# Seven block products in a second tile of a hybrid attention and recurrence kernel, with the weight sums made by accumulating DMAs

## The chip, the cores and the metric

The kernel runs on one core of a Trainium2 chip, in one launch. The metric is the device time in microseconds of that core, the median of three runs; one more execution was profiled. The engines are TensorE (PE), VectorE (DVE), ScalarE (ACT), GpSimd (POOL) and SyncE (SP), which only issues DMAs here.

## The reference

One block of a streaming encoder over `x` (1, 2048, 1024), all in float32. Eight attention heads with 2 key heads, over a window of two chunks of 64 positions, with sinks; four heads of a gated linear recurrence (HGRN2) with a 128 x 128 state; each branch gated by SiLU:

```python
h = rmsnorm(x, w_norm_pre[l])
proj = h @ w_in[l]                                   # 1024 -> 3328 = 26 * 128
q_a, k_a, v_a, z_a, q_r, f_r, i_r, z_r = jnp.split(proj, SPLIT_POINTS, axis=-1)
...
o_a = sliding_window_sink_attention(q_a, k_a, v_a, attn_sinks[l]) * jax.nn.silu(z_a)
...
o_r = hgrn2_chunkwise(q_r, f_r, i_r, lb)
o_r = rmsnorm(o_r, hgrn_norm[l]).reshape(B, S, HGRN_WIDTH) * jax.nn.silu(z_r)
y = jnp.concatenate([o_a, o_r], axis=-1) @ w_out[l]  # 1024 -> 1024
x = x + rmsnorm(y, w_norm_post[l])
```

## The kernel before

**Tiles and steps.** The sequence is cut into four tiles of 512 positions (`TILES`, `N`), numbered 0 to 3, worked one after the other. A tile has 26 weight tiles of 128 output columns for the input projection (key, value, 4 query, 4 gate, and forget, query, value, gate of each of four heads) and then the output projection, whose weight is 8 more weight tiles (`OUT0` to `WT` = 34). Each engine runs through the same numbered steps `s`, one per weight tile, and does the part of attention or recurrence that is due; `between` (L729) places TensorE's small matmuls among the products.

**Split weights and operands.** A float32 product is made of three matmuls of float32r operands: high by high, low by high, high by low (`products`, L591). So each weight tile (512 KB) has a high and a low half. ScalarE makes the high half (`split_hi`, L919), VectorE the low half (`split_lo`, L1257) from the raw tile that SyncE loaded (`load_raw`, one of 4 slots of `w_raw`). A weight tile of the input projection is 24 matmuls.

**Keeping the halves.** `SPLIT_SLOT` says in which of 4 slots of `w_hi`, `w_lo` a weight tile lies; the last six of tile 0 use slots 0, 1, 2 alone. With `LATE` = 6, the first six weight tiles are split in tile 0 without being saved; those from 6 on are saved to DRAM (`save_split`, `kept_hi` and `kept_lo`); the first six of tile 1 are loaded raw and split again, and saved then. From `FRESH` = 40 on, `load_split` (L461) loads both halves back. It waits that TensorE has finished with the slot (`wait_slot`) and that the slot's saves have landed (`wait_saved`, L379). SyncE's program is in order, so whatever follows a wait in it waits too; at each weight tile it comes to: raw load, save of the tile four back, load of kept halves, then x, tables, sums, residual, stores.

**Two forms of the output projection.** Tiles 0 and 1 (`t < FAST`, FAST = 2) multiply plainly: 8 weight tiles x 24 = 192 matmuls of 512 columns (`out_plain`). Tiles 2 and 3 use a 2 x 2 block form with seven products rather than eight: 56 units x 3 = 168 matmuls (`out_fast`, `UNITS`). It needs sums of activation blocks (`sum_head`, `a_sum`; VectorE), their high and low parts, and eight further weight tiles T1 to T4, which are sums of blocks of the output weight. These are made once: SyncE loads four raw tiles, VectorE subtracts them four times (`sum_weights`, L1453), ScalarE rounds them to high halves that lie in `mix_hi`, `mix_lo` (`sums_high`), VectorE makes the low halves, SyncE saves both. The first four are made at the end of tile 1, the other four in steps 5 to 8 of tile 2.

**Attention.** In step 8, 10, 12, 14 TensorE computes the scores of a pair of chunks (`scores`), VectorE takes the maximum and writes `probs` (`softmax_first`, L1426), ScalarE the exponent, VectorE sums and scales it one step later (`softmax_sums`, L1434), and TensorE transposes it two steps after the scores (`turn`, L643).

**End of a tile.** After a plain tile ScalarE squares the output, VectorE and GpSimd scale it and add the residual, and ScalarE issues five DMAs that store it (`PLAIN_STORES`, L1232). GpSimd issues no DMA.

Of the kernel before, what the change touches and what calls it, by code (L numbers as in the profile page):

```python
# [49 lines left out]
OUT0 = H0 + 4 * HEADS  # L50
WT = OUT0 + KT
# [10 lines left out]
FAST = 2  # L62
# [6 lines left out]
SPLIT_SLOT += [w % 4 for w in range(WT)] + [(WT + w) % 4 for w in range(FAST_WT)] * (TILES - FAST)  # L69
assert WT == 34 and OUT0 == 26 and FAST_WT % 4 == 0 and FAST == 2  # L70
# [40 lines left out]
SUMS_IN = (FAST - 1, H0 + 8), (FAST, 5)  # L111
SUMS_OUT = ((FAST, 0, 0), (FAST, 1, 2)), ((FAST, H0, 0), (FAST, H0 + 2, 2))
SUMS_AT = 5
# [39 lines left out]
LATE = 6  # L153
# [36 lines left out]
def hybrid_block(nc, x, x_rows, weights, cos, sin, vectors, w_post, squares, out, kept):  # L190
# [3 lines left out]
    with ctx:  # L194
# [3 lines left out]
        def sem(name):  # L198
# [32 lines left out]
        t_probs = nc.alloc_sbuf_tensor_at("t_probs", [P, 2, 2, N], FP32R, offset=probs_at)  # L231
        t_more = nc.alloc_sbuf_tensor_at("t_more", [P, 2, 2, N], FP32R, offset=raw_at + 4 * RAW_SLOTS * KT * P)
# [38 lines left out]
        t_hi = [t_more[:, 0, :, :], t_probs[:, 1, :, :], t_more[:, 1, :, :], t_probs[:, 0, :, :]], \  # L271
               [mix[:, 2 * i:2 * i + 2, :] for mix in (mix_hi, mix_lo) for i in range(2)]
# [32 lines left out]
        stored = [sem(f"stored{i}") for i in range(2)]  # L305
# [38 lines left out]
        t_raw, t_sum, t_high, t_low, t_saved = (sem(n) for n in ("t_raw", "t_sum", "t_high", "t_low", "t_saved"))  # L344
# [27 lines left out]
        def wait_raw(engine, i):  # L372
            engine.wait_ge(w_loaded[i % RAW_SLOTS], 16 * (i // RAW_SLOTS + 1))

# [58 lines left out]
        def _(sp):  # L433
            def load_x(tile, k):


                if k == 0:
                    sp.wait_ge(h_lo_done.sem, h_lo_done.after(tile - 1, -1))
                    sp.wait_ge(x_squared.sem, x_squared.after(tile - 1, -1))
                    sp.wait_ge(finished.sem, finished.after(tile - 2, -1))  # L440
                    sp.wait_ge(finished_pool.sem, finished_pool.after(tile - 2, -1))
                sp.dma_start(x_in[:, k:k + 2, :],
                             x[bass.ts(tile, P), k * N:(k + 2) * N].rearrange("p (k n) -> p k n", n=N)).then_inc(x_quarter[k // 2], 16)
# [17 lines left out]
            def load_split(tile, w):  # L461
# [4 lines left out]
                if w == P7A and tile == FAST:  # L466
                    sp.wait_ge(t_saved, 16 * 2 * T_TILES)
# [4 lines left out]
            def load_sums(j):  # L472

                if j == 0:
                    sp.wait_ge(lo_split.sem, lo_split.after(0, 0) + FRESH - 1)
                else:
                    sp.wait_ge(t_saved, 16 * T_TILES)
                for r, w in enumerate((B11, B21, B12, B22)):
                    sp.dma_start(w_raw[:, r, :, :], weights[(w + j) * P:(w + j + 1) * P, :].rearrange("p (k m) -> p k m", k=KT)).then_inc(t_raw, 16)

            def save_sums(j, first):

                sp.wait_ge(t_high, 4 * j + first + 2)
                sp.wait_ge(t_low, 4 * j + first + 2)
                for r, w in ((0, T1), (2, T3)) if first == 0 else ((3, T2), (1, T4)):
                    rows = slice((w + j) * P, (w + j + 1) * P)
                    sp.dma_start(kept[0][rows, :].rearrange("p (k m) -> p k m", k=2), t_hi[j][r].bitcast(FP32)).then_inc(t_saved, 16)
                    sp.dma_start(kept[1][rows, :].rearrange("p (k m) -> p k m", k=KT), w_raw[:, r, :, :]).then_inc(t_saved, 16)
# [44 lines left out]
            for t in range(TILES):  # L533
                for w in range(tiles_of(t)):
# [12 lines left out]
                    if w - H0 in range(0, KT, 2) and t + 1 < TILES:  # L547
                        load_x(t + 1, w - H0)
                    if w == OUT0 and t + 1 < TILES:
                        load_tables(t + 1)  # L550
                    if (t, w) in SUMS_IN:
                        load_sums(SUMS_IN.index((t, w)))
                    for j in range(2):
                        for first in (0, 2):
                            if (t, w, first) in SUMS_OUT[j]:
                                save_sums(j, first)
# [10 lines left out]
            sp.wait_ge(stored[0], 32 * TILES + 48)  # L567
            sp.wait_ge(stored[1], 48 * TILES + 32)
# [336 lines left out]
        def _(act):  # L905
# [98 lines left out]
            def sums_high(k):  # L1004

                act.wait_ge(t_sum, k + 1)
                if k == 4:
                    act.wait_ge(t_saved, 16 * T_TILES)
                r = (0, 2, 3, 1)[k % 4]
                act.activation(t_hi[k // 4][r], w_raw[:, r, :, :].rearrange("p k m -> p (k m)").rearrange("p (k n) -> p k n", k=2), ACT.Copy).then_inc(t_high, 1)  # L1010
# [30 lines left out]
            for t in range(TILES):  # L1041
                links[0] = 0
                for s in range(WT):
# [63 lines left out]
                    for head in range(HEADS):  # L1107
                        if s == out_step(head) + 2:
                            act.wait_ge(head_mixed.sem, head_mixed.after(t, head))
                            act.activation(mix_hi[:, QT + head, :], h_mix[:, :], ACT.Copy).then_inc(mixh_hi.sem, 1)  # L1110
                        if t >= FAST and s == out_step(head) + (3 if head < HEADS - 1 else 2):
                            act.wait_ge(s_made.sem, s_made.after(t, head))
                            if t == FAST and head == 0:
                                act.wait_ge(t_saved, 16 * 2 * T_TILES)
                            act.activation(s_hi[:, :, head, :], s_tmp, ACT.Copy).then_inc(s_high.sem, 1)
                    if t == FAST and s in (SUMS_AT + 1, SUMS_AT + 2):
                        for k in range(2):
                            sums_high(4 + 2 * (s - SUMS_AT - 1) + k)
# [15 lines left out]
                    for head in range(HEADS):  # L1134
                        if s == out_step(head):
# [4 lines left out]
                            act.wait_ge(o_done.sem, o_done.after(t, head))  # L1140
                            act.activation(o_sq_hi, out_b, ACT.Square)
# [27 lines left out]
                    if t >= FAST and s in MIXA:  # L1169
                        first = MIXA[s][0] == 0  # L1170
                        act.wait_ge(gated.sem, gated.after(t, PAIRS - 1)) if first else act.wait_ge(a_sum.sem, a_sum.after(t, 0))
                        if t == FAST and first:
                            act.wait_ge(t_saved, 16 * 2 * T_TILES)
# [9 lines left out]
                    if s == OUT0 + 4 and t < FAST:  # L1183
                        for b in range(4):
                            square_y(t, 0, b)
                        for k in range(4) if t == FAST - 1 else ():
                            sums_high(k)
# [34 lines left out]
                if t + 1 < TILES:  # L1222
# [4 lines left out]
                    for b, cols, pieces, pool_pieces in PLAIN_STORES if t < FAST else ():  # L1227

                        act.wait_ge(finished.sem, finished.after(t, pieces - 1))
                        if pool_pieces:  # L1230
                            act.wait_ge(finished_pool.sem, finished_pool.after(t, pool_pieces - 1))
                        act.dma_start(out[bass.ds(t * N + b * P, P), cols[0] * N:(cols[-1] + 1) * N].rearrange("p (h n) -> p h n", n=N),  # L1232
                                      q_gate[:, 2 * b + cols[0]:2 * b + cols[-1] + 1, :]).then_inc(stored[b // 2], 16)
# [4 lines left out]
        def _(dve):  # L1238
# [77 lines left out]
            def rope_turn(t, r):  # L1316
# [14 lines left out]
                else:  # L1331
                    dve.wait_ge(stored[0], t * 32 + 32)
# [71 lines left out]
            def softmax_first(t, q):  # L1404
# [15 lines left out]
                dve.wait_ge(turned.sem, turned.after(t, q - 1))  # L1420
                if t == 0 and q == 0:
# [22 lines left out]
            def sum_head(t, h):  # L1444
# [3 lines left out]
                dve.tensor_tensor(s_tmp[:, S2, :], h_mix[:, 2 * P:], s3[:, h, :], ALU.subtract).then_inc(s_step, 1)  # L1448
# [361 lines left out]
```

## Time and profile before

| | |
|---|---|
| runs | 864.86 us median of 3 (864.5 to 866.69) |
| the profiled execution's own time | 864.57 us |
| its span, first to last instruction | 862.7 us |
| granted TensorE clock | 0.999 of full |
| TensorE busy | 851.9 us (99%) |
| VectorE busy | 631.9 us (73%) |
| ScalarE busy | 519.0 us (60%) |
| GpSimd busy | 114.6 us (13%) |
| DMA | 211.20 MB, mean 245 GB/s |

Busy is the time in which an engine works on an instruction; matmuls overlap one another in it (one of 512 columns is shown with 0.39 us, and the next begins 0.23 us after it). All times below are counted from the first instruction of the span. A tile has 816 such matmuls, or 792 with seven products, and runs for some 210 us.

### The profile page before, as it was taken

Reading aid. Unit: us, or ns where it says so; the run is one execution under the profiler, and the core shown is the slowest. Engines: PE = TensorE matmul, PEld = TensorE weight load, DVE = VectorE, ACT = ScalarE, POOL = GpSimd, SP = SyncE. Lnnn points to the kernel's source line nnn. Section 1 sums busy time; section 2 is a strip of 40 time slices with the busy share of each in tenths; the row PEclk is TensorE's granted clock in tenths of the full one; section 3 lists DMA queues with packets and bytes.
Section 4 is the critical chain, followed back from the end, with each engine's and each line's share of the span. In section 5 each row is a group of like instructions: output and inputs, shape, how many; then the busy total and the mean of one; then the engine's idle time right before and its main releaser. Section 6 shows DMA issues by size and latency. Waiting matters only on the chain.

```text
span 862.7 us, 12445 instructions
## 1 busy us (share of the span) xinstructions
PE 851.9 (99%) x4428; PEld 700.6 (81%) x4428; DVE 631.9 (73%) x1125; ACT 519.0 (60%) x1033; POOL 114.6 (13%) x84
## 2 busy tenths in 40 slices
PE   8999999999999999999999999999999999999997
PEld 6787788888888778888888878888888887888885
DVE  6878878674656799767747789887775368888846
ACT  7766445763466458567446655865853755576544
POOL 0000013430200000332020000144300000004220
PEclk9999999999999999999999999999999999999999
DMA  8686755748986647464898785445699674444586
GB/s 322 212 325 221 244 205 170 285 147 314 418 342 248 213 145 265 152 210 133 321 382 348 276 330 172 146 151 216 241 374 396 228 273 147 147 147 158 189 326 254
DMA packets 59981, 211.20 MB, mean 245 GB/s; under 512 B 6672, under 2 KB 6928, under 8 KB 59920
## 3 DMA queue, kind: packets, MB, share of 16 engines
q1 hardware_dynamic: 57904, 205.56, 65.3%
q10 hardware_dynamic: 2016, 4.85, 1.4%
q8 instruction: 35, 0.57, 0.3%
q14 instruction: 26, 0.21, 0.1%
HBM read 157.95 MB, written 52.43 MB: 244 GB/s over the span
## 4 chain that ended last, share of the span: by engine, by line
PE 84%; DVE 9%; ACT 4%; issue 3%; DVEq 0%
PE bank L596 55%; PE bank L605 5%; PE turn_b L852 3%; PE score_b L852 3%; PE bank L852 3%; PE score_b L605 3%; PE turn_b L605 3%; PE turn_b L653 2%; DVE kv_tok L1386 2%; PE score_b L629 2%; PE turn_b L706 2%; PE bank L697 1%; PE bank L687 1%; PE turn_b L709 1%; ACT probs_t L951 1%
## 5 line engine op out<-in xcount | busy, mean ns | idle before, releaser
L596 PE MATMUL bank<-h_hi,w_lo 128*128 128x512 f32 x832 | 326.9, 393 | 0.0
L596 PE MATMUL bank<-h_lo,w_hi 128*128 128x512 f32 x832 | 326.3, 392 | 0.0
L596 PE MATMUL bank<-h_hi,w_hi 128*128 128x512 f32 x832 | 324.4, 391 | 0.5 <-issue 0.5
L596 PEld LDWEIGHTS bank<-h_lo,w_hi 128*128 128x128 f32 x832 | 156.4, 188 | 34.7 <-issue 3.3
L596 PEld LDWEIGHTS bank<-h_hi,w_hi 128*128 128x128 f32 x832 | 156.4, 188 | 33.1 <-issue 1.0
L596 PEld LDWEIGHTS bank<-h_hi,w_lo 128*128 128x128 f32 x832 | 156.3, 188 | 32.8
L1716 POOL TENSOR_TENSOR mix_lo<-v_r,mix_hi 128x512 fp32r<-128x512 f32 x16 | 21.2, 1322 | 539.0 <-ACT v_r L1142 539.0
L1263 DVE TENSOR_TENSOR w_lo<-w_raw,w_hi 128x1024 fp32r<-128x1024 f32 x36 | 44.8, 1248 | 34.6 <-ACT w_hi L924 34.1
L1386 DVE STREAM_TRANSPOSE kv_tok<-k_mid 32x128 f32<-32x128 f32 x192 | 58.1, 303 | 2.8
L924 ACT ACTIVATE w_hi<-w_raw 128x1024 fp32r<-128x1024 f32 x38 | 39.8, 1051 | 24.9 <-issue 10.2
L1700 POOL TENSOR_TENSOR x_acc<-x_acc,x_sq 128x512 f32<-128x512 f32 x21 | 32.7, 1557 | 70.0 <-ACT x_sq L974 70.0
L928 ACT ACTIVATE g_a<-g_b 128x512 f32<-128x512 f32 x30 | 18.9, 630 | 38.2 <-DVE g_b L1340 38.2
L939 ACT ACTIVATE g_a<-g_a 128x512 f32<-128x512 f32 x32 | 20.2, 632 | 34.6 <-DVE g_a L1344 34.6
L1068 ACT ACTIVATE f_b<-bank 32x512 f32<-32x512 f32 x48 | 28.3, 589 | 15.6 <-PE bank L596 9.7
L960 ACT ACTIVATE kv_tok<-f_d 32x128 f32<-32x128 f32 x96 | 29.5, 307 | 10.0 <-DVE f_d L1580 8.9
L1344 DVE SCALAR_TENSOR_TENSOR g_a<-g_b,g_a 128x512 f32<-128x512 f32 x30 | 21.7, 723 | 18.3 <-ACT g_a L930 18.3
L960 ACT ACTIVATE probs<-f_d 32x128 f32<-32x128 f32 x96 | 29.5, 307 | 1.2
L1637 DVE TENSOR_TENSOR_SCAN f_c<-reset,f_b 128x512 f32<-128x512 f32 x16 | 19.6, 1225 | 11.3 <-ACT f_b L1125 11.3
L1479 DVE SCALAR_TENSOR_TENSOR q_gate<-q_gate,y_stats,x_in 128x512 f32<-128x512 f32 x28 | 23.1, 873 | 4.4 <-DMA x_in<-in_x_rows 3.5
L605 PE MATMUL bank<-w_hi,mix_lo 128*128 128x512 f32 x64 | 25.3, 395 | 0.0
L605 PE MATMUL bank<-w_hi,mix_hi 128*128 128x512 f32 x64 | 24.9, 390 | 0.0
L605 PE MATMUL bank<-w_lo,mix_hi 128*128 128x512 f32 x64 | 24.9, 389 | 0.0
(280 smaller groups left out, 1549.2 us busy)
## 6 DMA issues: line engine op xcount, KB each, us to landing
w_hi<-kept_hi SPq DMA_DIRECT2D x108, 512.0 KB, 3.8
w_lo<-kept_lo SPq DMA_DIRECT2D x108, 512.0 KB, 4.9
w_raw<-in_weights SPq DMA_DIRECT2D x46, 512.0 KB, 6.2
kept_hi<-w_hi SPq DMA_DIRECT2D x34, 512.0 KB, 6.3
kept_lo<-w_lo SPq DMA_DIRECT2D x34, 512.0 KB, 7.4
x_in<-in_x_rows SPq DMA_DIRECT2D x8, 1024.0 KB, 8.1
x_in<-in_x SPq DMA_DIRECT2D x15, 512.0 KB, 6.6
kept_lo<-w_raw SPq DMA_DIRECT2D x8, 512.0 KB, 7.0
```

The lines of the kernel that those rows point to most:

```text
L596: mm = pe.matmul(acc(w)[:, :], stationary[:, s, k, :], moving[:, k, :], start=(m == 0), stop=(m == 3 * KT - 1), skip_group_check=True)
L605: mm = pe.matmul(y_bank[half][b][:, :], mix[:, k, b * P:(b + 1) * P], weight[:, SPLIT_SLOT[index(t, w)], (k % 2) * 4:(k % 2) * 4 + 4, :].r ...
L852: mm = pe.matmul(into, mix, weight, start=w in (P1A, P7A, P2A, P4A) and k == 0 and part == 0, stop=k == KT // 2 - 1 and part == 2, skip_gr ...
L924: act.activation(w_hi[:, SPLIT_SLOT[i], :, :], w_raw[:, i % RAW_SLOTS, :, :], ACT.Copy).then_inc(hi_split.sem, 1)
L960: copy = act.activation(square(v_tok(t, h), j, i), square(f_d[:, :], i, j), ACT.Copy)
L1068: copy = act.activation(dst[32 * b:32 * b + 32, :], acc(s - 1)[32 * (b ^ 1):32 * (b ^ 1) + 32, :], ACT.Copy)
L1263: dve.tensor_tensor(w_lo[:, s, :, :], w_raw[:, i % RAW_SLOTS, :, :], w_hi[:, s, :, :], ALU.subtract).then_inc(lo_split.sem, 1)
L1344: dve.scalar_tensor_tensor(g_a[:, :], g_b[:, :], 0.0, gate_log(t, i), ALU.min, ALU.subtract).then_inc(gate_arg.sem, 1)
L1386: last = dve.transpose(square(kv_tok[:, 0, :], j, i), square(k_mid[:, :], i, j))
L1479: dve.scalar_tensor_tensor(y, y, y_scale[:, b:b + 1], x_in[:, 2 * b + half, :], ALU.mult, ALU.add).then_inc(finished.sem, 1)
L1700: pool.tensor_tensor(x_acc[:, :], x_acc[:, :], x_sq[:, :], ALU.add).then_inc(x_added.sem, 1)
L1716: pool.tensor_tensor(o_sq_lo, o_sq[:, :], o_sq_hi, ALU.subtract).then_inc(o_low.sem, 1)
```

## The change

- `FAST` is 1: tile 1 uses the seven-product form too. Only tile 0 multiplies plainly.
- `LATE` is 0: all 34 weight tiles are saved in tile 0, and tile 1 loads kept halves from its first weight tile on. No raw tile is loaded or split after tile 0.
- The sums T1 to T4 are made in DRAM (`t_rows`): GpSimd issues, in steps 8 to 19 of tile 0 (`SUMS_MADE`), two copies of weight rows, two accumulating DMAs, and two times a copy of the last sum and an accumulation onto it; 1 MB each, each waiting for an earlier one. The signs differ from before, so some activation sums and one product change sign (`sum_head`, `post`).
- SyncE loads the eight sum tiles (`load_sum`: two in tile 0, six in steps 4 to 9 of tile 1), ScalarE and VectorE split one each in steps 2 to 9 of tile 1, and GpSimd saves the halves, two DMAs for each, when TensorE is done with weight tile 3, 4, 6, 7, 9, 10, 12, 13 of tile 1 (`SUMS_OUT`). Two of the eight lie in the memory of `probs` and `probs_t`, so VectorE's first softmax write of tile 1 waits for their saves (`probs_saved`).
- GpSimd, no longer ScalarE, issues the stores of tile 0's output.
- The loads of the next tile's x come three weight tiles later (`X_AT`).

```diff
-FAST = 2
+FAST = 1
+LATE = 0
...
+SUMS_IN = {(FAST - 1, OUT0): (0, 1), (FAST, 4): (2,), (FAST, 5): (3,), (FAST, 6): (4,), (FAST, 7): (5,), (FAST, 8): (6,), (FAST, 9): (7,)}
+SUMS_SPLIT = {2 + k: (k,) for k in range(T_TILES)}
+SUMS_OUT = (3, 4, 6, 7, 9, 10, 12, 13)
+SUMS_MADE = {8: (0, None), 9: (1, None), 10: (0, B12), 11: (1, B12), 13: (2, None), 15: (2, B11), 17: (3, None), 19: (3, B21)}
+X_AT = H0 + 3
...
+            def load_sum(k):
+
+                sp.wait_ge(t_made[k // 2], 16)
+                if k == 2:
+                    sp.wait_ge(weighed.sem, weighed.after(FAST - 1, PAIRS - 1))
+                    sp.wait_ge(head_mixed.sem, head_mixed.after(FAST - 1, HEADS - 1))
+                if k >= 4:
                     sp.wait_ge(lo_split.sem, lo_split.after(0, 0) + FRESH - 1)
+                sp.dma_start(t_in[k], t_rows[k * P:(k + 1) * P, :].rearrange("p (k m) -> p k m", k=KT)).then_inc(t_loaded[k], 16)
...
                     if LATE + RAW_SLOTS <= i <= FRESH:
                         save_split(i - RAW_SLOTS)
-                    if i == FRESH + 1:
-                        for late in range(FRESH + 1 - RAW_SLOTS, FRESH):
-                            save_split(late)
+                    if FRESH <= i < FRESH + 3:
+                        save_split(i - 3)
                     if i >= FRESH:
                         load_split(t, w)
+                    for k in SUMS_IN.get((t, w), ()):
+                        load_sum(k)
...
+            def sum_high(k):
+
+                act.wait_ge(t_loaded[k], 16)
+                act.activation(t_hi[k], t_in[k].rearrange("p k m -> p (k m)").rearrange("p (k n) -> p k n", k=2), ACT.Copy).then_inc(t_high, 1)
...
                 dve.wait_ge(turned.sem, turned.after(t, q - 1))
+                if t == FAST and q == 0:
+                    dve.wait_ge(probs_saved, 64)
...
+            def sum_low(k):
+
+                dve.wait_ge(t_high, k + 1)
+                dve.tensor_tensor(t_in[k], t_in[k], t_hi[k].rearrange("p k n -> p (k n)").rearrange("p (k m) -> p k m", m=P), ALU.subtract).then_inc(t_low, 1)
...
+            def save_sum(k):
+
+                pool.wait_ge(t_low, k + 1)
+                pool.wait_ge(tile_done.sem, tile_done.after(FAST, SUMS_OUT[k]))
+                rows, saved = slice((WT + k) * P, (WT + k + 1) * P), probs_saved if k in (2, 3) else t_saved
+                pool.dma_start(kept[0][rows, :].rearrange("p (k m) -> p k m", k=2), t_hi[k].bitcast(FP32)).then_inc(saved, 16)
+                pool.dma_start(kept[1][rows, :].rearrange("p (k m) -> p k m", k=KT), t_in[k]).then_inc(saved, 16)
...
+            def make_sum(s):
+
+                n, added = SUMS_MADE[s]
+                dst, src = t_rows[n * 2 * P:(n + 1) * 2 * P, :], (B11, B22)[n] if n < 2 else None
+                pool.wait_ge(lo_split.sem, lo_split.after(0, s))
+                if added is not None:
+                    pool.wait_ge(t_base, 16 * (n + 1 + (n == 0)))
+                    pool.dma_start(dst, weights[added * P:(added + 2) * P, :], accum_op=ALU.add, max_dma_last_dim=4 * KT * P).then_inc(t_made[n], 16)
+                elif n < 2:
+                    pool.dma_start(dst, weights[src * P:(src + 2) * P, :]).then_inc(t_base, 16)
+                else:
+                    pool.wait_ge(t_made[n - 1], 16)
+                    pool.dma_start(dst, t_rows[(n - 1) * 2 * P:n * 2 * P, :]).then_inc(t_base, 16)
+
             for t in range(TILES):
+                for k in range(T_TILES) if t == FAST else ():
+                    save_sum(k)
```

## Rows read from the trace of the kernel before

**Rows 1.** The page: busy us (share of the span) xinstructions.

```profile
PE 851.9 (99%) x4428; PEld 700.6 (81%) x4428; DVE 631.9 (73%) x1125; ACT 519.0 (60%) x1033; POOL 114.6 (13%) x84
```

**Rows 2.** The waits, TensorE: us in total, times, longest us.

```profile
PE bank L861 <- DVE ones_r L1265: 3.5, 1, 3.5
```

**Rows 3.** The chain of waits, in order of time: start us, us, what.

```profile
24.98 29.04 PE bank L596 x128
...
214.21 1.36 PE bank L605 x6
...
226.45 10.88 PE bank L596 x48
...
237.78 33.55 PE bank L596 x148
...
284.62 0.49 PE turn_b L643 x16
...
439.97 10.88 PE bank L596 x48
...
649.11 10.88 PE bank L596 x48
```

**Rows 4.** Stretches: length, busy us by engine (x), PEclk, DMA share, GB/s.

```profile
0.00:22.00 22.00, 18.07 (x77) 15.25 (x78) 14.24 (x24) 16.13 (x25) 1.67 (x9) 1.00 0.90 324
...
196.00:226.00 30.00, 30.00 (x134) 24.86 (x133) 12.09 (x17) 10.83 (x18) 0.00 (x0) 1.00 0.95 370
226.00:270.00 44.00, 44.00 (x195) 36.43 (x195) 28.46 (x37) 30.41 (x66) 5.74 (x4) 1.00 0.91 351
```

**Rows 5.** Timeline of ScalarE in the entry: start us, us, instruction.

```profile
21.11 1.05 ACT L924 ACTIVATE w_hi<-w_raw 128x1024 fp32r<-128x1024 f32 x1
```

**Rows 6.** Timeline of VectorE in tile 0: low halves of weights 4, 11, 19, 31.

```profile
24.77 1.23 DVE L1263 TENSOR_TENSOR w_lo<-w_raw,w_hi 128x1024 fp32r<-128x1024 f32 x1 [0.27 <-issue]
...
60.23 1.23 DVE L1263 TENSOR_TENSOR w_lo<-w_raw,w_hi 128x1024 fp32r<-128x1024 f32 x1 [0.19 <-ACT w_hi L924]
...
119.18 1.23 DVE L1263 TENSOR_TENSOR w_lo<-w_raw,w_hi 128x1024 fp32r<-128x1024 f32 x1
...
208.21 1.22 DVE L1263 TENSOR_TENSOR w_lo<-w_raw,w_hi 128x1024 fp32r<-128x1024 f32 x1 [6.49 <-ACT w_hi L924]
```

**Rows 7.** Timeline of GpSimd, its first instruction after the setup.

```profile
126.83 1.29 POOL L1716 TENSOR_TENSOR mix_lo<-v_r,mix_hi 128x512 fp32r<-128x512 f32 x1 [124.01 <-ACT v_r L1142]
```

**Rows 8.** DMAs issued at 196.8 us: KB each, us from issue to landing.

```profile
x_in<-in_x_rows SPq DMA_DIRECT2D x1, 1024.0 KB, 5.9
```

**Rows 9.** DMAs issued from 207 to 212 us.

```profile
kept_lo<-w_lo SPq DMA_DIRECT2D x1, 512.0 KB, 11.0
```

**Rows 10.** DMAs issued from 61.4 to 62.7 us, a burst of three.

```profile
w_raw<-in_weights SPq DMA_DIRECT2D x1, 512.0 KB, 4.2
...
kept_lo<-w_lo SPq DMA_DIRECT2D x1, 512.0 KB, 5.9
```

**Rows 11.** DMAs issued from 270 to 271 us, a pair, after weight 7 of tile 1.

```profile
w_lo<-kept_lo SPq DMA_DIRECT2D x1, 512.0 KB, 4.9
```

**Rows 12.** DMAs issued at 26 us, one alone.

```profile
w_raw<-in_weights SPq DMA_DIRECT2D x1, 512.0 KB, 3.3
```

**Rows 13.** The waits, SyncE's queue: us in total, times, longest us.

```profile
SPq L382 <- DMA kept_lo<-w_lo: 9.6, 4, 5.6
```

**Rows 14.** Timeline of VectorE, first softmax of tile 1 and of tile 2.

```profile
274.01 1.22 DVE L1426 TENSOR_TENSOR probs<-score_b,s_stats 128x1024 f32<-128x1024 f32 x1
...
279.68 1.23 DVE L1434 TENSOR_TENSOR probs<-probs,s_stats 128x1024 f32<-128x1024 f32 x1
...
487.73 1.22 DVE L1426 TENSOR_TENSOR probs<-score_b,s_stats 128x1024 f32<-128x1024 f32 x1
...
495.48 1.23 DVE L1434 TENSOR_TENSOR probs<-probs,s_stats 128x1024 f32<-128x1024 f32 x1
```

**Rows 15.** DMAs issued from 203 to 204 us.

```profile
kept_lo<-w_lo SPq DMA_DIRECT2D x1, 512.0 KB, 13.8
```

More of the change, by code:

```diff
@@ L150, in splits @@
     return [t * WT + w for w in split_at(s) if 3 < t * WT + w < FRESH]
-LATE = 6
 FRESH = WT + LATE
@@ L187, in after, with hybrid_block @@
         return self.per_tile + (sum(self.sizes[:tile]) if tile >= 0 else tile * self.per_tile) + i + 1
-def hybrid_block(nc, x, x_rows, weights, cos, sin, vectors, w_post, squares, out, kept):
+def hybrid_block(nc, x, x_rows, weights, cos, sin, vectors, w_post, squares, out, kept, t_rows):
     ctx = ExitStack()
@@ L440, in load_x @@
                     sp.wait_ge(finished.sem, finished.after(tile - 2, -1))
-                    sp.wait_ge(finished_pool.sem, finished_pool.after(tile - 2, -1))
+                    sp.wait_ge(finished_pool.sem, finished_pool.after(tile - 2, -1) if tile != FAST + 1 else finished_pool.after(FAST - 1, 1))
                 sp.dma_start(x_in[:, k:k + 2, :],
@@ L1109, in _ @@
                             act.wait_ge(head_mixed.sem, head_mixed.after(t, head))
+                            if t == FAST and head == 0:
+                                act.wait_ge(t_saved, 32 * (T_TILES - 2))
                             act.activation(mix_hi[:, QT + head, :], h_mix[:, :], ACT.Copy).then_inc(mixh_hi.sem, 1)
@@ L1140, in _ @@
                             act.wait_ge(o_done.sem, o_done.after(t, head))
+                            if t == FAST and head == 0:
+                                act.wait_ge(probs_saved, 64)
                             act.activation(o_sq_hi, out_b, ACT.Square)
@@ L1226, in _ @@
                         split_hi(i)
[L1227 to L1233, printed above, removed]
             assert links[0] == act_step.per_tile, links[0]
@@ L1650, in _ @@
                             sum_head(t, h)
-                    if t == FAST and 0 <= s - SUMS_AT < 4:
-                        sum_weights(1, s - SUMS_AT)
-                    for i in splits(t, s) if (t, s) != (1, 0) and (t or kind not in (0, 1)) else ():
+                    for k in SUMS_SPLIT.get(s, ()) if t == FAST else ():
+                        sum_low(k)
+                    for i in splits(t, s) if t or kind not in (0, 1) else ():
                         if i in DVE_LOW:
@@ L1660, in _ @@
                         dve.tensor_scalar(y_bias[:, :], y_sq[:, 0:4], 1.0 / D_MODEL, EPS, ALU.mult, ALU.add).then_inc(y_biased.sem, 1)
-                        for part in range(4) if t == FAST - 1 else ():
-                            sum_weights(0, part)
                 if t >= FAST:
@@ L1670, in _ @@
                         dve.tensor_tensor(mix_lo[:, 0, :], x_acc[:, :], mix_hi[:, 0, :], ALU.subtract).then_inc(x_low, 1)
-                    if b == 3 and t == 0:
-                        for i in splits(1, 0):
-                            split_lo(i)
                     copy_y(t, 1, b)
@@ L1712, in _ @@
                     h_of, kind = divmod(s - 1 - H0, 4) if H0 < s <= OUT0 else (0, None)
+                    if t == 0 and s in SUMS_MADE:
+                        make_sum(s)
                     for h in range(HEADS):
@@ L1748, in _ @@
                     pool.tensor_tensor(y, y, x_in[:, 2 * b, :], ALU.add).then_inc(finished_pool.sem, 1)
+                for b, cols, pieces, pool_pieces in PLAIN_STORES:
+                    pool.wait_ge(finished.sem, finished.after(t, pieces - 1))
+                    if pool_pieces:
+                        pool.wait_ge(finished_pool.sem, finished_pool.after(t, pool_pieces - 1))
+                    pool.dma_start(out[bass.ds(t * N + b * P, P), cols[0] * N:(cols[-1] + 1) * N].rearrange("p (h n) -> p h n", n=N),
+                                  q_gate[:, 2 * b + cols[0]:2 * b + cols[-1] + 1, :]).then_inc(pool_stored[b // 2], 16)
 def weight_tiles(w_in, w_out):
@@ L1806 @@
     kept = [nc.dram_tensor(f"kept_{part}", ((WT + T_TILES) * P, KT * P), FP32, kind="Internal").ap() for part in ("hi", "lo")]
-    hybrid_block(nc, *aps, out, kept)
+    t_rows = nc.dram_tensor("t_rows", (T_TILES * P, KT * P), FP32, kind="Internal").ap()
+    hybrid_block(nc, *aps, out, kept, t_rows)
     got = run_bass_kernel_spmd(nc, [arrays], core_ids=[0]).results[0]["out"]
```

105 lines of the change are left out of this document (36 added, 69 removed).

## The prediction

> **What bounds the kernel now.** I read the page's busy times first: TensorE is busy 851.9 us, 99% of the span [rows 1], and the list of waits shows nearly none on it: its longest is 3.5 us ahead of the first matmul [rows 2]. So every microsecond must come from fewer matmuls, and every late operand costs its full delay. The chain of waits then gives the length of each tile, since each tile begins with the same piece of 48 matmuls: tile 1 (eight block products) runs from 226.45 to 439.97 = 213.52 us, tile 2 (seven) to 649.11 = 209.14 us [rows 3]. Six 512-column matmuls take 1.36 us there, 0.227 each, and a weight tile of 24 takes 5.44. Last I read the DMA queues and the tile boundary, since the change lives there: from 196 to 226 us the DMA engines are 95% busy, then 91% up to 270 [rows 4].
>
> **Products.** Tile 1 loses 24 of its 192 output matmuls, 24 x 0.227 = 5.44 us. What the seven-product form really gives here is the difference between the two tiles, 213.52 - 209.14 = 4.38 us; the 1.06 between is VectorE's and GpSimd's extra work showing as small gaps in tile 2, and tile 1 will have the same extra work. Tile 2 is relieved of the weight sums (eight of VectorE's subtractions of 1.2 us, as long as a low half [rows 6]), which I credit with 0.2. Bounds: 4.38 and 5.44; I take **-4.6**.
>
> **Entry.** Six more weight tiles are saved in tile 0, 6 MB from about 13 us on, into queues that are 90% busy over the first 22 us [rows 4]. The half of weight 4 now waits for the save of weight 0. In the old run ScalarE made the high half at 21.11 [rows 5] and VectorE the low half at 24.77 to 26.0 [rows 6]; the chain's piece from 24.98 [rows 3] holds the last 3 matmuls of weight 2 and then weight 3, so TensorE reaches weight 4 at 24.98 + 27 x 0.227 = 31.1 and 5 us are spare. At 0.5 MB per 1.3 us (a burst's step, below) the save of weight 0 lands near 20 and each later one stays just ahead of its half. I take 0, bounds 0 and 2. The raw splits that leave tile 1's start were hidden; nothing is gained by that.
>
> **Accumulating DMAs.** GpSimd issues eight 1 MB DRAM-to-DRAM transfers in tile 0, paced by the low halves of weights 8 to 19, and each waits for an earlier one. No such transfer is in the trace. GpSimd has no other work before 126.83 [rows 7]. The low half of weight 11 is ready at 61.5 and that of weight 19 at 120.4 [rows 6]; four transfers in sequence lie between, so each may take some 15 us. A 1 MB load took 5.9 [rows 8], and with a second read I put an accumulation at 12 at most. Cost 0; if they took 25 each, GpSimd's low half of the head squares would be late by tens of us and the kernel slower by as much, for which I keep a small chance.
>
> **Boundary of tiles 0 and 1: the save-load chain.** This is the first real cost. Tile 1's weights 0, 1, 2 used to be loaded raw and split; they now come from DRAM, in the slots that weights 31, 32, 33 leave, and SyncE's load waits until that slot's last save has landed. SyncE's order is save 31, load 0, save 32, load 1, save 33, load 2: a wait on landing in every link, each holding up the next save. Step by step:
> - The low half of weight 31 is done at 209.43 [rows 6], its save is issued from 209.8 on, and the low part's landed 11.0 us after its issue at 210.3, so at 221.3 [rows 9]. Two raw loads ahead of it go away (1.25 us each), so 218.8.
> - Load 0 is issued then and save 32 behind it: a burst of three 0.5 MB transfers, issued about 0.4 apart, landed its first after 4.2 us and its third 6.7 us after the first issue (5.9 + 0.8) [rows 10], a fourth comes 1.2 later: load 0 at 224.1 (due 226.3, fine), save 32 at 226.6.
> - Load 1 is issued at 226.7; its pair lands 4.9 + 0.4 = 5.3 after [rows 11], at 232.0. Due 226.3 + 5.44 = 231.7: 0.3 late.
> - Save 33 lands at 226.7 + 7.8 = 234.5, load 2 at 239.8. TensorE is due there at 237.8 [rows 3], 238.1 with the delay above: 1.7 late.
> - The 2 MB of tile 0's output stores fall into 230 to 238. At a burst's step of 1.25 us per 0.5 MB they take 5 us of the engines; the chain has idle latency of 2 to 3 us per link that they can use, so I add 1.3.
> Together **+3.3**. Bounds: 0, if landings are as short as the 3.3 us of a lone load in the entry [rows 12]; 7, if the stores come wholly before load 2 (5 us for them instead of 1.3). That such waits on a landing happen is in the old trace: SyncE waited four times for a kept_lo save before a load, 5.6 us at most [rows 13]; there TensorE needed the tile over 10 us later, here at once.
> [...]
>
> **Softmax of tile 1: the wait for GpSimd's transfers.** The sums of index 2 and 3 sit in the area of the probabilities, and VectorE's first write there (L1426, step 8) now waits for their saves. GpSimd issues the last pair only when weight 7 is done, which is 270.4 (SyncE's load with the same kind of wait is issued between 270 and 271 [rows 11]). The old run had no GpSimd DMA. As SyncE's: a save pair together with the load pair that SyncE issues at the same moment is a burst of four, 7.8 us; I add 0.8 for the issue of two and the engine's start: landing at about 279.0. VectorE wanted to write at 274.01 and ended the normalising 6.9 us later, at 280.9 [rows 14]; TensorE transposes at 284.62 [rows 3]. With one low half in between (in tile 2, with two, the same stretch is 487.73 to 496.71, 9.0 [rows 14]) it is 7.9, so 286.9: **+2.2**. Bounds: 0, if the pair lands by 276.7 (a pair alone takes 5.3); 7.4, if it lands after the 13.8 us seen in the busiest stretch [rows 15], at 284.2, 5.2 later than I take. Queued behind that VectorE instruction are the gate steps and the read-outs of the projection banks, which TensorE needs four weights later (20 us): no second cost. ScalarE's exponent waits too, but is in this same chain.
> [...] No GpSimd DMA is in this trace.
>
> **The rest.** ScalarE and VectorE get 1.05 and 1.22 us more in each of steps 2 to 9 of tile 1; tile 2 already bore two at a time with one wait of 0.2 us. Stores from GpSimd must have landed before VectorE's query write, which needs TensorE's weight 2 of tile 1 (done at 243) and a swap by ScalarE, and are there by about 245 against 254 for the write. The loads of x three steps later still come steps ahead of their squares. The sign changes keep the instruction count. All 0.
>
> **Sum.** The profiled execution took 864.57 (span 862.70 and 1.87 around it), 0.3 under the median of the runs, 864.86. 864.57 - 4.6 + 3.3 + 2.2 = 865.5, on the median **865.8**. About 0.3% (2.6 us) is what a measurement tells from no change: faster is under 862.3, slower over 867.4.
>
> **Rivals.**
> A, the waits are hidden: transfers land quicker than my bursts, say the boundary costs 1 and the softmax 0 to 1. For it: both costs are differences of a few us out of 10-us chains, and SyncE alone never made TensorE wait. Against it: the queues are at 91 to 95% just there. 864.9 - 4.6 + 1.5 = **861.8**, and 860.3 with nothing lost. Chance 0.29.
> B, the likeliest, both waits show at about my sizes: 862.3 to 867.4. Chance 0.43.
> C, slower: GpSimd's transfers become the bound. [...] It decides from the point at which the pair takes over 10.5 us from the end of weight 7. For it: 13.8 us was seen [rows 15]; 2.2 MB per step (1 MB load, 0.5 MB sum, 0.7 MB save) in 5.44 us is 400 GB/s in steps 4 to 9, the rate of a queue that is never empty. Against it: the load issued then landed in 4.9, so the queues had drained by then in the old run [rows 11]. With slow accumulations (also GpSimd's), chance 0.28.
> That the change doesn't do what it says would show as 192 output products in tile 1; the diff leaves no room for it.
>
> Range 8 in 10: 860.9 to 870.5. B alone: 863 to 867.5.
>
> **What would show it.** Tile 1 from its first to its last matmul against 209; TensorE idle just before weight 1 and 2 of tile 1, released by kept-row loads, 3 us in total; SyncE waiting on kept_lo saves three times around 218 to 235; VectorE idle ahead of L1426's successor in tile 1 step 8 by about 5 us, and TensorE idle by 2 before the transpose of the first pair. Wrong if TensorE runs through either place without a gap, or if it idles in tile 0 (entry, or head sums behind GpSimd).

## The result and the profile after

The changed kernel took 876.45 us (median of 4 runs, 875.43 to 877.82) against 865.03 for the kernel before on the same chip (4 runs): ratio 1.0129, 95% interval [1.0113, 1.0144]. It is slower by 1.3%, and the time lies above the range of the prediction (860.9 to 870.5). The profiled span is 874.1 us against 862.7, so some 11.3 us are to be found. On the page TensorE's busy time hardly moved, although 24 matmuls are gone: 1.9 us more than in [rows 1] for 24 instructions fewer.

```profile
PE 853.8 (98%) x4404; PEld 699.7 (80%) x4404; DVE 627.8 (72%) x1135; ACT 519.2 (59%) x1035; POOL 130.9 (15%) x110
```

So part of the loss is idle time, and part is matmuls that take longer. The list of waits of TensorE (us in total, times, longest) shows three new ones of over 1 us; before, only the entry had one of that size [rows 2].

```profile
PE turn_b L585 <- DMA w_lo<-kept_lo: 3.5, 1, 3.5
...
PE turn_b L644 <- issue: 3.4, 1, 3.4
PE bank L597 <- DMA w_lo<-kept_lo: 1.8, 1, 1.8
PE bank L698 <- DVE a_t L1348: 0.6, 3, 0.2
```

The chain of waits now leaves TensorE before the end of tile 0. From 210 to 245 us it runs over SyncE and its DMAs, where before it held TensorE's matmuls alone [rows 3]: save of weight 31, save of weight 32, save of weight 33, load of weight 2, each issued when the one before it had landed. Columns: start us, us, what.

```profile
210.29 8.44 DMA kept_lo<-w_lo
...
220.12 7.67 DMA kept_lo<-w_lo
...
229.19 8.53 DMA kept_lo<-w_lo
...
238.14 7.11 DMA w_lo<-kept_lo
...
245.29 0.50 PE turn_b L585
...
246.13 35.06 PE bank L597 x148
...
282.28 11.11 PE bank L597 x48
...
294.48 3.37 issue
297.85 1.11 PE turn_b L644 x16
298.96 6.14 PE bank L597 x16
...
451.51 10.88 PE bank L597 x48
...
660.48 10.88 PE bank L597 x48
```

Three things are to be read here. Tile 2 starts 451.51 - 439.97 = 11.54 us later than before [rows 3], and tile 2 itself takes 208.97 (209.14 before): the loss lies in tile 1 and ahead of it. The piece of 148 matmuls took 33.55 us before and 35.06 now: the same work, 1.5 slower. And in step 10 TensorE is idle for 3.37 us before the transpose (L644). The profile names no releaser for that wait, but VectorE's timeline does for its own, two steps earlier: the first softmax write of tile 1 stood still for 5.19 us until the save of a sum had landed.

```profile
289.63 1.23 DVE L1418 TENSOR_TENSOR probs<-score_b,s_stats 128x1024 f32<-128x1024 f32 x1 [5.19 <-DMA kept_lo<-t_probs]
```

The stretches show why the same matmuls are slower. PEclk is the granted clock as a share: it is 1.00 in most stretches, and 0.72, 0.60 and 0.53 in those just behind the three gaps.

```profile
227.00:234.00 7.00, 5.61 (x25) 4.32 (x23) 6.56 (x8) 3.14 (x9) 5.60 (x7) 1.00 0.75 208
234.00:240.00 6.00, 5.55 (x17) 4.43 (x18) 0.00 (x0) 1.03 (x2) 0.55 (x1) 0.72 1.03 421
240.00:246.00 6.00, 2.49 (x11) 1.68 (x11) 0.00 (x0) 0.00 (x0) 0.00 (x0) 0.98 1.01 393
246.00:250.00 4.00, 4.00 (x13) 3.17 (x12) 2.34 (x4) 2.27 (x3) 0.00 (x0) 0.60 1.02 414
...
300.00:304.00 4.00, 4.00 (x11) 3.10 (x10) 3.93 (x6) 2.06 (x4) 0.00 (x0) 0.53 0.36 147
```

At 1.00 a matmul begins 0.227 us after the one before it; the timeline shows 0.43 in these stretches, here behind the first gap (start us, us, instruction, idle before it):

```profile
234.45 0.50 PE L597 MATMUL bank<-h_hi,w_hi 128*128 128x512 f32 x1 [1.84 <-DMA w_lo<-kept_lo]
...
236.28 0.63 PE L597 MATMUL bank<-h_hi,w_hi 128*128 128x512 f32 x1
236.71 0.63 PE L597 MATMUL bank<-h_hi,w_lo 128*128 128x512 f32 x1
```

The start of every weight tile on TensorE, after against before, gives the balance of the two spans. Entry: +0.7. Weights 0 to 3 of tile 1: +9.15. Step 10 (the first softmax of tile 1): +6.2. Later gaps in tile 1: +0.9. Tile 1's output product: -5.44. Tile 2: -0.2. Sum +11.3.

### The profile page after: what moved, and what is told of

Read it like the earlier page. It is cut to its first block, busy times and chain, and to the rows that moved or that the text cites. A ratio compares the mean times of both kernels' runs of the same rounds, so it can differ in the third digit from the quotient of the medians.

```text
span 874.1 us, 12467 instructions
## 1 busy us (share of the span) xinstructions
PE 853.8 (98%) x4404; PEld 699.7 (80%) x4404; DVE 627.8 (72%) x1135; ACT 519.2 (59%) x1035; POOL 130.9 (15%) x110
## 4 chain that ended last, share of the span: by engine, by line
PE 63%; DVE 17%; ACT 8%; issue 6%; DMA 5%; SPq 1%; POOL 0%; DVEq 0%; ACTq 0%
PE bank L597 43%; PE turn_b L853 4%; PE score_b L853 4%; PE bank L853 4%; DVE kv_tok L1376 4%; DMA kept_lo<-w_lo 3%; PE score_b L630 2%; ACT probs_t L952 1%; PE turn_b L654 1%; DMA w_raw<-in_weights 1%; DVE f_c L1623 1%; PE turn_b L707 1%; ACT probs L961 1%; PE turn_b L710 1%; PE bank L698 1%
## 5 line engine op out<-in xcount | busy, mean ns | idle before, releaser
L1253 DVE TENSOR_TENSOR w_lo<-w_raw,w_hi 128x1024 fp32r<-128x1024 f32 x30 | 37.6, 1255 | 25.5 <-ACT w_hi L925 25.1
L925 ACT ACTIVATE w_hi<-w_raw 128x1024 fp32r<-128x1024 f32 x32 | 33.6, 1051 | 13.3 <-issue 7.4
L1243 DVE SCALAR_TENSOR_TENSOR h_lo<-x_in,vec,h_hi 128x512 fp32r<-128x512 f32 x32 | 24.1, 799 | 2.4 <-ACT h_hi L979 2.3
L1330 DVE TENSOR_TENSOR g_b<-bank,x_scale 128x512 f32<-128x512 f32 x32 | 21.8, 682 | 3.5 <-PE bank L597 3.1
L1157 ACT ACTIVATE v_win<-g_a 32x128 f32<-32x128 f32 x48 | 14.8, 308 | 14.2 <-DVE g_a L1540 13.5
## 6 DMA issues: line engine op xcount, KB each, us to landing
kept_lo<-w_lo SPq DMA_DIRECT2D x34, 512.0 KB, 11.3
t_rows<-in_weights POOLq DMA_DIRECT2D x4, 1024.0 KB, 13.2
```

What stands on the lines that cost most here:

```text
L925: act.activation(w_hi[:, SPLIT_SLOT[i], :, :], w_raw[:, i % RAW_SLOTS, :, :], ACT.Copy).then_inc(hi_split.sem, 1)
L1243: dve.scalar_tensor_tensor(h_lo[:, k, :], x_in[:, k, :], w_pre[:, k:k + 1], h_hi[:, k, :], ALU.mult, ALU.subtract).then_inc(h_lo_done.sem, 1)
L1253: dve.tensor_tensor(w_lo[:, s, :, :], w_raw[:, i % RAW_SLOTS, :, :], w_hi[:, s, :, :], ALU.subtract).then_inc(lo_split.sem, 1)
L1330: dve.tensor_tensor(g_b[:, :], acc(w)[:, :], x_scale[:, :], ALU.mult).then_inc(tile_read.sem, 1)
```

## The experiments

All start from the changed kernel. Experiments 1 to 4 shared their runs of the kernel before (865.25 us), and 5 to 8 theirs (865.03); each ratio is against these. Nothing is left out of the computation in any of them.

**1. Saves ahead of the loads.** The save of weight 32 is issued before load 0 and that of 33 before load 1, so that no save waits behind a load that itself waits for a landing.

```diff
-                    if FRESH <= i < FRESH + 3:
-                        save_split(i - 3)
+                    if i == FRESH:
+                        save_split(FRESH - 3)
+                        save_split(FRESH - 2)
+                    if i == FRESH + 1:
+                        save_split(FRESH - 1)
```

> The changed kernel with one edit: SyncE issues the saves of weights 31 and 32 together ahead of tile 1's load 0, and save 33 ahead of load 1, so that no load's wait on a landing holds up the next save. Theory P (the serial chain of save, landing, load makes TensorE idle before weights 1 and 2 of tile 1, and each idle stretch is followed by matmuls at the lower clock): weights 1 and 2 start without a gap, the 9.15 us lost there come back, 867.3 us. Rival D (the DMA engines are simply full at the boundary, whatever the order): the gaps stay in sum, within 2 us of 876.4. The softmax gap in step 10 stays in both, some 6 us.

Measured 866.95 us (10 runs), ratio 1.0020 [1.0011, 1.0030]; span 864.7, 9.4 less than the changed kernel's. TensorE's waits at weights 1 and 2 are gone, and the 9.15 us with them: against the kernel before, weight 3 starts no later than weight 0 does (0.32 us each). The softmax is left:

```profile
PE turn_b L647 <- issue: 3.6, 1, 3.6
...
PE turn_b L657 <- ACT probs_t L1078: 0.9, 1, 0.9
```

The DMAs were not faster (load 1 took 8.6 us to land where the changed kernel's took 6.2), only earlier. So the boundary's loss came of the order of issue, as P had it, and not of full DMA engines (D).

**2. And the saves of sums 2 and 3 earlier.**

```diff
-SUMS_OUT = (3, 4, 6, 7, 9, 10, 12, 13)
+SUMS_OUT = (3, 4, 5, 5, 9, 10, 12, 13)
```

> As before, and GpSimd also issues the saves of the two sums that lie in the softmax memory when weight 5 is done instead of 6 and 7. Theory P: both gaps go, 876.4 - 9.15 - 6.24 = 861.1 us, under the kernel before. Rival D (transfers moved together only shift the fullness): VectorE still waits in step 8, or a kept load comes late elsewhere in steps 4 to 8; 864 to 868.

Measured 861.89 us (10 runs), ratio 0.9967 [0.9955, 0.9979]; span 860.0: faster than both kernels, by 0.3% than the one before. The wait before L647 is gone. VectorE still waited 0.75 us for the saves in step 8, as D had it, but the time is near P's. And step 10 still costs 1.8 us, in a wait that the prediction did not have, before the second group of matmuls that read the turned probabilities:

```profile
PE turn_b L657 <- ACT probs_t L1078: 1.7, 1, 1.7
```

**3. TensorE kept at work through its gaps.** Throw-away matmuls (9, 16 and 15 of 512 columns) run where it would stand idle; the waits stay, now behind them.

```diff
+WARM = {1: 9, 2: 16}
...
+                if t == FAST and q == 0:
+                    pe.wait_ge(tile_read.sem, tile_read.after(t, 7))
+                    for i in range(15):
+                        pe.matmul(bank[3][:, :], ones_r[:, :], h_hi[:, 0, :], start=True, stop=True)
...
+                    if t == FAST and w in WARM:
+                        pe.wait_ge(y_read.sem, y_read.after(t, (2, 3, 1, 7)[w] - 8))
+                        for i in range(WARM[w]):
+                            pe.matmul(acc(w)[:, :], ones_r[:, :], h_hi[:, 0, :], start=True, stop=True)
                     wait_split(pe, t, w)
```

> The changed kernel with its waits left as they are, and TensorE kept busy with throw-away matmuls of 512 columns just ahead of the three waits of tile 1: 9 ahead of weight 1 (2.0 us), 16 ahead of weight 2 (3.6 us), 15 ahead of the first transpose of the probabilities (3.4 us). Theory P, in which an idle stretch is followed by matmuls at half clock: the waits are filled, the slow matmuls after them (some 3.8 us at the boundary, 2.9 us in step 10) go: 869.8 us, 868 to 872. Rival W (the idle time alone is the loss and the low clock comes from something else, as the DMA load): 876 or more.

Measured 876.22 us (4 runs), ratio 1.0128 [1.0112, 1.0143], no better than the changed kernel: my P failed. The fills did what they should to the clock: it stayed at 1.00 up to 304 us, and no matmul behind a fill was slow. Stretches, then the timeline of TensorE:

```profile
234.00:240.00 6.00, 4.85 (x21) 3.86 (x21) 0.00 (x0) 0.59 (x2) 0.00 (x0) 1.00 1.02 418
...
246.00:250.00 4.00, 3.96 (x17) 3.27 (x18) 1.69 (x3) 2.27 (x3) 0.00 (x0) 1.00 1.03 420
304.00:312.00 8.00, 7.14 (x28) 5.40 (x29) 5.77 (x10) 4.37 (x7) 1.06 (x2) 0.79 0.35 88
```

```profile
240.94 3.79 PE L893 MATMUL bank<-h_hi,ones_r 128*128 128x512 f32 x16
246.04 0.50 PE L586 MATMUL turn_b<-mix_hi,ones_r 128*128 128x512 f32 x1 [1.31 <-DMA w_lo<-kept_lo]
...
304.86 1.08 PE L659 MATMUL turn_b<-probs_t,v_win 128*64 128x256 f32 x8 [2.53 <-ACT probs_t L1084]
```

Weight 2 starts when its load lands (246.0), whether TensorE came to it slowly or fast. The slow matmuls of weight 1, and those between L644 and L654 in step 10, stood in front of waits that were longer than they; take them away and the same time becomes idle. Only the slow matmuls of weight 2 had nothing behind them to hide in: they took 6.99 us in the changed kernel and 5.49 here, 1.5 less. The whole did not gain them. In this profiled execution load 2 landed 1.3 us later than in the changed kernel's (counted from weight 0), and in step 10 the 2.53 us wait, hidden until now, came out, and the clock fell behind it. So the low clock is some 1.5 of the 11.3 us, read from weight 2's own matmuls, and the landings are most of the rest. Rival W was right about the time, but not that the low clock comes from something else: with TensorE filled and the DMA engines as busy (share 1.02) the clock stayed up.

**4. GpSimd's stores later.** Its five output stores of tile 0 wait until weight 1 of tile 1 is done.

```diff
+                pool.wait_ge(tile_done.sem, tile_done.after(FAST, 1))
                 for b, cols, pieces, pool_pieces in PLAIN_STORES:
```

> The changed kernel with GpSimd's five stores of tile 0's output held back until weight 1 of tile 1 is done (some 8 us later), SyncE's chain as it was. Rival S (the stores beside the chain make load 2 late): save 33 lands near 234.5 instead of 237.7 and load 2 near 240 instead of 245.2, the gap before weight 2 goes and about 5.5 us with it: 871. The gap before weight 1 stays, since load 1 is issued before any store. Theory P without contention (the chain alone makes both gaps): at most 2 us come back, 874 to 876.

Measured 873.95 us (4 runs, 872.01 to 874.85), ratio 1.0096 [1.0078, 1.0114]; the profiled execution (872.01, span 870.2) was the quickest of the four, and the places below are of that one. Load 2, issued with nothing of GpSimd's in the queues, landed after 4.6 us instead of 7.11:

```profile
w_lo<-kept_lo SPq DMA_DIRECT2D x1, 512.0 KB, 4.6
```

```profile
232.20:234.30 2.10, 0.03 (x2) 0.02 (x1) 1.16 (x2) 2.02 (x4) 0.00 (x0) 1.00 1.02 417
234.00:240.00 6.00, 5.72 (x24) 4.43 (x24) 0.00 (x0) 0.62 (x2) 0.00 (x0) 1.00 0.49 182
236.00:237.00 1.00, 1.00 (x6) 0.84 (x5) 0.00 (x0) 0.00 (x0) 0.00 (x0) 1.00 0.01 4
240.00:241.75 1.75, 0.02 (x1) 0.00 (x1) 0.00 (x0) 0.00 (x0) 1.43 (x3) 1.00 0.91 339
```

The chain now has a stretch in which nearly nothing moves, between the data of save 33 and the start of load 2 (236 to 237 us, share 0.01); from 234 to 240 the DMA engines are half idle, where the changed kernel kept them at 1.03. In TensorE's own two waits they are busy with the loads that it waits for (1.02 and 0.91). So without the stores a good part of the loss is latency in sequence, and the loads come late because they are issued late. The boundary cost 4.4 us instead of 9.15. Late landings that the stores had made are gone (1.3 in the save of weight 33, 2.5 in load 2: 3.8 us), and so are the slow matmuls of weight 2 (1.5); the chain itself began some 0.7 us later here, counted from weight 0. Some 4.4 us are the chain without the stores.

The median tells less: 2.5 us come back, where P said at most 2 and S 5.5. Part of the 4.75 us was lost again even in this execution: 0.8 at weights 6 and 7, where TensorE waited for a load, and 0.5 in step 10. And the three slower runs had a mean granted clock of 0.992 to 0.995 against 0.997 in the profiled one (0.990 to 0.992 in the changed kernel's four); that the slow matmuls were back in them is likely, but no trace shows it. S is right that the stores make load 2 late, but the gap before weight 2 only shrank, from 3.5 to 1.7 us.

**5. One sum's split out of step 9's program.**

This edit stands on those of experiments 1 and 2.

```diff
-SUMS_SPLIT = {2 + k: (k,) for k in range(T_TILES)}
+SUMS_SPLIT = {2 + k: (k,) for k in range(T_TILES - 1)} | {12: (7,)}
```

> Base: the version with both repairs (861.9 us, span 860.0). In it TensorE still waited 1.74 us in step 10 for ScalarE's probs_t copy, although the probs were free in time; there VectorE did the low half of sum 7 (1.23 us, behind ScalarE's 1.04 us high half) ahead of g_b, and ScalarE's copy for the turn stands behind the gate that waits for g_b. This kernel splits sum 7 three steps later, in step 12 (beside weight 13, which has no turn). Theory Q (the sum's split in step 9's program is what is left of the softmax's loss): the 1.74 us wait is gone, step 10 to 11 as before, about 860.1 us (span 858.2). Rival (the wait is the turn of tile 1 as such, or the split makes the same wait where it now stands): 861.9 +-0.4.

Measured 860.97 us (6 runs, 859.91 to 863.81), ratio 0.9956 [0.9944, 0.9968]; the lowest median here, though its interval overlaps experiment 2's. Its span of 859.3 holds an entry 0.6 us longer than the base's. Step 10 now costs 0.4 instead of 1.8:

```profile
PE turn_b L657 <- ACT probs_t L1078: 0.4, 1, 0.4
```

The time alone does not decide, as it lies between Q's 860.1 and the rival's 861.5; the wait does: most of it went, and none of its size came up where the split now stands. Q holds for 1.4 of the 1.8 us. What the last 0.4 is stays open. In the base (experiment 2) VectorE's timeline shows the sum's low half between the normalising and the read-out that releases ScalarE's gate, and ScalarE's copy for the turn stands behind that gate:

```profile
282.51 1.22 DVE L1429 TENSOR_TENSOR probs<-probs,s_stats 128x1024 f32<-128x1024 f32 x1
...
285.99 1.23 DVE L1451 TENSOR_TENSOR w_raw<-w_raw,mix_lo 128x1024 f32<-128x1024 f32 x1 [0.16 <-ACT mix_lo L1011]
287.13 0.68 DVE L1333 TENSOR_TENSOR g_b<-bank,x_scale 128x512 f32<-128x512 f32 x1
```

```profile
289.83 1.02 ACT L1078 ACTIVATE probs_t<-turn_b 128x1024 f32<-128x1024 f32 x1
```

**6 and 7. LATE back at 6.** Weights 0 to 5 of tile 1 are raw tiles split again; run 7 has the earlier saves of sums 2 and 3 too.

```diff
-LATE = 0
+LATE = 6
```

> The changed kernel with LATE back at 6: weights 0 to 5 of tile 1 come from raw tiles split again, as in the kernel before, and their halves are saved in tile 1; all else of the change stays. Theory P (the 9.15 us at the tile boundary are the loads of saved halves that wait for their saves and share the queues with GpSimd's stores): no wait at weights 1 and 2, the entry's +0.7 gone too, step 10's +6.2 stays: about 866.6 us. Rival D (VectorE then has six low halves and the sums' splits in the same steps 0 to 9 and becomes late, or the sums' loads into the raw area come late): 869 to 874 us. Rival W (the loss at the boundary is GpSimd's five stores as such): 872 or more.

> LATE at 6 as in the other run and GpSimd's saves of sums 2 and 3 after weight 5 instead of 6 and 7. Theory P: 866.6 less the 4.4 us that the earlier saves gave back elsewhere (4.7 in the spans with and without them), 862.2 us. Rival D: the sums' splits slip behind the low halves, so that the earlier saves are not earlier: 865 or more.

Measured 869.19 us (ratio 1.0046 [1.0033, 1.0059]) and 868.91 (1.0046 [1.0032, 1.0061]), 4 runs each. At weights 0 to 3 the loss fell from 9.15 to 1.6 us, so that part of P holds; 1.3 of what is left is a wait for VectorE's low half, as rival D had it. Rival W is out: GpSimd's stores are where they were. But 4.9 us were lost anew at weight 8, where six saves of 1 MB now stand in tile 1 among the loads of sums and weights; and step 10 cost 2.1 us instead of the 6.2 that P kept. The time is at the low end of rival D. TensorE's waits of run 6:

```profile
PE bank L597 <- DMA w_lo<-kept_lo: 3.0, 1, 3.0
PE turn_b L654 <- ACT probs_t L1075: 2.0, 1, 2.0
PE turn_b L585 <- DVE w_lo L1253: 1.3, 1, 1.3
```

The 3.0 us are new, at weight 8 (issue to landing of a loaded low half between 262 and 290 us: 10.8, in the changed kernel 8.2), and 1.7 of slow matmuls follow them. In run 7 the earlier saves did their work: step 10 cost nothing any more. (Sum 7's split still stood in step 9 there; that it did no harm is presumably due to the 1.7 us of slow matmuls in weight 8, which give VectorE and ScalarE that much more time.) But its wait at weight 8 grew to 3.9 us, and in the profiled execution the entry was 1.4 us longer than in run 6, so that the spans differ by 0.6 and the medians by 0.3. My P for it missed by 6.7 us. The time is rival D's, but not for its reason, since the saves were indeed earlier; the loss sits in the queues at weight 8.

**8. Pauses made on purpose.** On the version of experiment 2, GpSimd holds TensorE up before six weights, far from the change.

```diff
+PAUSES = {(2, 3): 3, (2, 5): 5, (2, 7): 9, (3, 3): 2, (3, 5): 4, (3, 7): 7}
...
+                    if (t, w) in PAUSES:
+                        pe.wait_ge(paused, 1 + list(PAUSES).index((t, w)))
                     wait_split(pe, t, w)
...
+                for (at, w), n in PAUSES.items():
+                    if at == t:
+                        pool.wait_ge(tile_done.sem, tile_done.after(t, w - 1))
+                        for i in range(n):
...
+                            pool.memset(pad[:, :], 0.0).then_inc(pad_step, 1)
...
+                        pool.sem_inc(paused, 1)
```

> The version with both repairs, plus six pauses of TensorE made on purpose before weights 3, 5 and 7 of tiles 2 and 3: TensorE waits for GpSimd, which after the previous weight runs 3, 5, 9 and 2, 4, 7 small memsets one after the other. Nothing is left out. Theory K (TensorE's granted clock falls after idle times from about 2 us and the matmuls behind a pause then run at the lower level): each pause costs its own length, and those over 2 us cost 1 to 2 us more in the next weight, whose 24 matmuls take over 5.44 us; windows behind them show a granted clock of 0.5 to 0.8. Rival (the low clock of the changed kernel came of the DMA traffic or of something else): every pause costs only its length, 24 matmuls 5.44 us behind each.

One run, 882.96 us. The stretches that begin near each pause's end, in the order of idle times 1.22, 1.95, 3.42, then 0.85, 1.58, 2.69 us:

```profile
457.00:462.00 5.00, 4.97 (x22) 4.11 (x23) 1.64 (x3) 4.44 (x11) 0.00 (x0) 1.00 0.93 381
470.00:475.50 5.50, 5.33 (x16) 4.33 (x17) 1.98 (x3) 1.86 (x6) 0.07 (x1) 0.69 0.40 161
486.40:491.50 5.10, 5.10 (x15) 4.05 (x16) 0.69 (x2) 0.63 (x1) 0.00 (x0) 0.67 0.15 59
676.00:681.00 5.00, 4.67 (x21) 3.87 (x22) 1.25 (x3) 4.58 (x12) 0.23 (x1) 1.00 1.01 409
689.00:694.00 5.00, 4.92 (x22) 4.08 (x23) 1.98 (x3) 2.15 (x6) 0.00 (x0) 1.00 0.47 188
702.90:708.00 5.10, 5.06 (x12) 4.00 (x13) 1.38 (x2) 0.70 (x2) 0.00 (x0) 0.50 0.80 308
```

The next 24 matmuls took 5.44 + 0.15, 1.75, 1.73, 0.13, 0.13 and 3.01 us. K holds: far from the change and with pauses as the only difference, idle time brings the clock down (the longest extra, 3.0 us, is above K's 1 to 2). A gap that does so costs 1.7 to 3 us more than its length, unless a wait behind it hides that (experiment 3). The rival's DMA traffic does not order them: behind the pauses of 1.22 and 0.85 us the clock stayed at 1.00 with shares of 0.93 and 1.01, and behind that of 3.42 it fell with 0.15.

## Why the prediction was wrong

The forecast was 865.8 us and the kernel took 876.45. Of the 10.6 us between them some 5.9 lie at the boundary of tiles 0 and 1, 4.0 in the softmax of tile 1 and 0.7 in the entry.

**Products, -4.6.** Right: -5.44 at the output product, +0.9 in later gaps of tile 1 (a_t, L698, the extra work named there), -0.2 in tile 2: -4.7.

**Entry, 0.** Measured +0.7, but the same step read between +0.2 and +1.8 in the experiments, and the two ends of that are reached with the same entry code (experiments 2 and 8). Without the six extra saves it read +0.2 and +1.5 (6 and 7). So no cost of the saves can be told from this scatter, and it stays under my bound.

**Accumulating DMAs, 0.** Right; from weight 3 to the end of tile 0 TensorE is late by the same 0.7 us throughout, so nothing waited for them. The page's list of DMAs has the accumulations (KB each, median us to landing); they took 12.1 to 14.7, over my 12 at most:

```profile
t_rows<-in_weights POOLq DMA_DIRECT2D x4, 1024.0 KB, 13.2
```

**Boundary, +3.3: the failed step.** The mechanism and its order were as forecast: the first save landed at 218.74 (218.8 forecast), and SyncE waited three times for a save where four shorter waits stood before [rows 13]:

```profile
SPq L393 <- DMA kept_lo<-w_lo: 23.3, 3, 8.1
```

What failed is the size of the links. I took loads 1 and 2 from a pair alone (4.9 [rows 11]), and the four transfers of a load with a save behind it from a burst of three with one more step (7.8 [rows 10]); here they took 9.0 and 9.9. Save of 32: landed 227.8, forecast 226.6. Load 1, with a save issued right behind it: 6.2 us to land instead of 4.9, so at 234.4 instead of 232.0. Save of 33: 237.7 instead of 234.5. Load 2: 7.1, at 245.25 instead of 239.8 plus 1.3 for the stores. So weight 1 came 2.0 us late instead of 0.3, weight 2 another 5.6 instead of 3.0, and weight 2's own matmuls took 1.5 longer, for which I had no term. The stores made 3.8 us of late landings in the one execution that can be compared (experiment 4), three times my 1.3; I had bounded them at 5 and then took a value near the low end. Load 2 landed in 4.6 us without GpSimd's stores and in 7.1 with them.

**The clock, a term left out.** [rows 2, 3] showed a TensorE without gaps, at 1.00 in all stretches read [rows 4]; I priced gaps by their length. The gap before weight 2 brought 1.5 us of slow matmuls, and the slow matmuls behind the other two gaps cost nothing more only because waits stood behind them (3.51 us before weight 2; 2.53 us in step 10, seen in experiment 3).

**Softmax, +2.2: mis-sized and one wait short.** Sum 3's save landed 9.4 us after weight 7 (forecast 8.6), and VectorE waited 5.2 us for it, as forecast (about 5); the wait at the transpose was 3.4. In the 8.6, the 0.8 for GpSimd's two issues and its start was my estimate, and no row showed the start; the two issues took 0.53 and 0.54 us. What I denied ("no second cost") came to 2.7 more: the next group that reads the turned probabilities was 7.2 us behind the transpose instead of 4.5 (284.45 and 288.91 before). In the changed kernel slow matmuls fill that time and only 0.2 us of it is idle; experiment 3, with the clock up, shows the wait of 2.53 us behind them. It is there since normalising, gate, sum's low half, read-out and ScalarE's gate stand in one line ahead of the copy. I had counted that low half before the normalising, not the one behind it. Experiments 2 and 5 separate two parts: 4.7 us of span for the late pair, 1.4 for the low half.

Rival C had the right sign, but not the reason: its pair landed after 9.4 us, under the 10.5 from which it decides, and the largest term is SyncE's order at the boundary, not GpSimd's transfers in the softmax. The 11.3 us are -4.7 + 0.7 + 9.15 + 6.2.

## What to carry to other kernels

When a kernel runs its main engine at 99%, a chain of "wait for a landing, issue, wait for the next" has to be priced with transfers of the busy stretch (links of 9.0 and 9.9 us here, where a burst elsewhere gave 7.8), and every save that only needs its data should be issued ahead of any load that has to wait (9.15 us came back in experiment 1). Follow a late operand past its first consumer: what stands behind it in the engines' programs can make a second wait that comes to light only when the first is mended (1.8 us in experiment 2). And before a slow stretch is called a cost, ask what wait it stands in front of.

## What the runs showed of the hardware that was not expected

- The granted clock fell behind idle times of 1.84 us (changed kernel), 1.95 (experiment 8) and all those of 2.5 to 3.95 us that were seen behind the entry. It did not behind any of 0.8 to 1.8 us, nor behind 2.01 us (run 6, step 10) and 2.08 us (experiment 4, before weight 1). So between 1.84 and 2.08 the length of the gap alone does not decide; what else does was not found.
- The low clock that followed (stretches of 0.50 to 0.79) cost 1.5 to 3 us in the next 24 matmuls (1.5 behind 3.51 us idle in the changed kernel; 1.75, 1.73 and 3.01 behind 1.95, 3.42 and 2.69 in experiment 8), in places as much as the gap itself.
- The low half of a load landed in 4.6 us with nothing ahead of it and no save or store beside it (experiment 4, load 2), in 6.2 with a save issued right behind it (changed kernel, load 1), in 7.1 among GpSimd's stores (its load 2) and in 8.6 behind a load and a save (experiment 1, load 1).
- An accumulating DMA of 1 MB from DRAM to DRAM took 13.2 us to land (median of 4), a plain one of the same size 7.3 to 7.5 (medians of 2), all issued by GpSimd in tile 0.
